# Hybrid decoder trunk, gated DeltaNet pairs: rows of the first pair fetched per head, pieces of the late gate product moved among the W and sample products

## The reference

```python
qkv = silu(causal_dwconv(h @ w_qkv, ...)); q, k = l2norm(q) * DK**-0.5, l2norm(k)
beta, g = sigmoid(ab[:8]), -exp(a_log) * softplus(ab[8:] + dt_bias)      # per head and token
# in chunks of 64 tokens (prompt) or 8 (sample), per head:
lmat = strict_lower(k_beta @ k.T * decay)
u, w = solve(lmat + I, [v*beta, k_beta*exp(gc)])                          # unit lower triangular
v_new = u - w @ S;  o = (q*exp(gc)) @ S + (q @ k.T * decay) @ v_new
S = S*exp(g_last) + (k*exp(g_last - gc)).T @ v_new
gate = silu(h @ w_g);  y = (rmsnorm(o) * gate) @ w_out
```

## Time and profile before

| | us |
|---|---|
| median of 3 runs | 1540.74 |
| lowest and highest run | 1536.88, 1546.56 |
| profiled execution, its own time | 1545.22 |
| its span, first to last instruction | 1543.5 |
| PE busy | 1513.7 (98%) |
| DVE, ACT, POOL busy | 796.0 (52%), 740.2 (48%), 1074.7 (70%) |
| mean granted TensorE clock | 0.986 |

### The profile page before, as it was taken

The page is one execution under the profiler, slowest core; times in us unless marked ns, Lnnn a source line. Parts: engine busy times, 40 slices in busy tenths (PEclk is TensorE's granted clock), DMA queues, the critical chain, the costliest instruction groups (busy, mean ns, idle before and its releaser), DMA issues.

```text
span 1543.5 us, 32205 instructions
## 1 busy us (share of the span) xinstructions
PE 1513.7 (98%) x10218; PEld 1475.3 (96%) x10218; DVE 796.0 (52%) x1788; ACT 740.2 (48%) x1412; POOL 1074.7 (70%) x1039
## 2 busy tenths in 40 slices
PE   9999999999999999999999999999899999999997
PEld 8999999998999999887999999999898899999997
DVE  4555554017555412996655531476767866555401
ACT  6654444445444434556644443457554535444332
POOL 5568887774776678984876767765656546777674
PEclk9999999999999999999999999999899989999999
DMA  6444444552544655221556545544422225444453
GB/s 241 123 135 146 157 153 145 149 159 83 163 140 159 160 149 172 83 83 60 166 157 163 146 128 150 177 149 123 138 89 88 81 82 180 150 149 149 119 153 109
DMA packets 88109, 212.47 MB, mean 138 GB/s; under 512 B 25600, under 2 KB 33312, under 8 KB 88032
## 3 DMA queue, kind: packets, MB, share of 16 engines
q1 hardware_dynamic: 88032, 211.49, 44.8%
HBM read 201.80 MB, written 9.66 MB: 137 GB/s over the span
## 4 chain that ended last, share of the span: by engine, by line
PE 88%; DVE 4%; issue 3%; POOL 2%; ACT 1%; DMA 1%; SPq 0%; DVEq 0%; POOLq 0%; ACTq 0%
PE bank L936 25%; PE bank L938 25%; PE bank L937 25%; PE bank L1339 2%; PE bank L1174 2%; PE bank L1350 1%; POOL wlo L639 1%; POOL wlo L641 1%; PE bank L1405 1%; PE bank L1290 1%; PE bank L1435 0%; DVE bank L2367 0%; DMA fst<-in_d_st 0%; PE bank L1199 0%; DMA tmp<-scr_g 0%
## 5 line engine op out<-in xcount | busy, mean ns | idle before, releaser
L639 POOL TENSOR_TENSOR wlo<-raw,whi 128x512 fp32r<-128x512 f32 (+3 forms) x394 | 452.4, 1148 | 376.6 <-ACT whi L1498 338.8
L936 PE MATMUL bank<-Gh,whi 128*128 128x320 f32 x1880 | 587.7, 313 | 3.1 <-DVE M L2349 2.0
L938 PE MATMUL bank<-Gh,wlo 128*128 128x320 f32 x1880 | 582.2, 310 | 0.0
L937 PE MATMUL bank<-Gl,whi 128*128 128x320 f32 x1880 | 582.0, 310 | 0.0
L641 POOL TENSOR_TENSOR wlo<-raw,whi 128x512 fp32r<-128x512 f32 (+3 forms) x394 | 473.2, 1201 | 0.0
L1498 ACT ACTIVATE whi<-raw 128x1024 fp32r<-128x1024 f32 (+3 forms) x396 | 370.6, 953 | 50.4 <-PE bank L938 37.4
L936 PEld LDWEIGHTS bank<-Gh,whi 128*128 128x128 f32 x1880 | 354.2, 188 | 5.4 <-DVE M L2349 2.2
L937 PEld LDWEIGHTS bank<-Gl,whi 128*128 128x128 f32 x1880 | 354.1, 188 | 1.1
L938 PEld LDWEIGHTS bank<-Gh,wlo 128*128 128x128 f32 x1880 | 353.9, 188 | 0.0
L936 PE MATMUL bank<-Hh,whi 128*128 128x320 f32 x912 | 283.7, 311 | 4.0 <-DVE Hl L2308 2.5
L938 PE MATMUL bank<-Hh,wlo 128*128 128x320 f32 x912 | 281.9, 309 | 0.0
(11 more groups left out here) (401 smaller groups left out, 1866.1 us busy)
## 6 DMA issues: line engine op xcount, KB each, us to landing
raw<-in_f_up SPq DMA_DIRECT2D x176, 512.0 KB, 3.4
raw<-in_f_down SPq DMA_DIRECT2D x64, 384.0 KB, 3.2
raw<-in_f_down SPq DMA_DIRECT2D x64, 320.0 KB, 3.2
raw<-in_c_pw SPq DMA_DIRECT2D x24, 512.0 KB, 3.6
raw<-in_a_in SPq DMA_DIRECT2D x16, 512.0 KB, 4.9
raw<-in_d_qk SPq DMA_DIRECT2D x16, 512.0 KB, 3.6
raw<-in_d_vg SPq DMA_DIRECT2D x16, 512.0 KB, 3.6
raw<-in_a_out SPq DMA_DIRECT2D x8, 512.0 KB, 3.5
```

The costliest lines, as they stand in the source:

```text
L639: pool.tensor_tensor(wlo[k][:, 0:half], raw[k][:, 0:half], whi[k][:, 0:half].bitcast(F32), ALU.subtract).then_inc(half_ready, 1)
L936: nc.tensor.matmul(dst, wh, h, start=start and n == 0, stop=False)
L937: nc.tensor.matmul(dst, wh, lo, start=False, stop=False)
L938: ins = nc.tensor.matmul(dst, wl, h, start=False, stop=stop and end and n == len(tiles) - 1)
```

## The change

Five things are moved.

1. **Rows.** For pair 0 the three row loads of head 0 wait for unit 10 of `d_vg`, those of head 1 for unit 11 (before: both for unit 11), and they stand ahead of the load of the first late gate's weights on SP. On ACT the high splits of units 10 to 12 stand at the end of the previous value instead of at the start of the next. The gate of head 6 is evicted and passed through silu after `differences` and `decays`.
2. **Gate pieces.** Of the 24 pieces per pair 16 instead of 24 are done by the end of the levels; four stand between the u products, two in each head's sample products.
3. **Banks.** Both heads' sample products and W of head 0 share bank 0; u of head 1 goes to bank 4, so that bank 5 belongs to the gate until its eviction.
4. **Eviction** of the gate (`late_evac`) moves from level 4 to the end of chunk step 2, and ACT's `gate_high`, `gated_late` move behind the next pair's `decays`.
5. **POOL.** `gate_low` moves from ahead of the state scaling to behind the sample spread (L753). In the last pair the split of the first `d_out` unit moves there too.

```diff
@@ SP
                         if x == 0:
                             sp.wait_ge(rows_stored, 48)
-                            sp.wait_ge(lo_ready, START["d_vg", 3] + 12)
+                        sp.wait_ge(half_ready, START["d_vg", 3] + 11 + x)
+                        sp.wait_ge(lo_ready, START["d_vg", 3] + 11 + x)
...
+                    gdn_row_loads(0)
                     load_gate(0)
-                    gdn_row_loads(0)
@@ POOL
-                if last:
-                    split_lo(START["d_out", 3] + 1, 1, UNIT)
-                else:
+                if not last:
                     scaled_keys(b + 1)
...
-                    gate_low(b + 1)
...
                                        ALU.mult).then_inc(vx_ready, 1)
+                if not last:
+                    gate_low(b + 1)
                 if not (isinstance(b, int) and b == 0):
                     head_lo(b * 2 - 2)
                 if last:
-                    for k in range(2, 4):
+                    for k in range(1, 4):
@@ PE
-                        gate(*((8, 9), (11, 12), (14, 15), (17, 18), (20, 24))[lev])
+                        gate(*((8, 9), (10, 11), (12, 13), (14, 15), (16, 16))[lev])
...
-                            gate(*((9, 11), (12, 14), (15, 17), (18, 20))[lev])
+                            gate(*((9, 10), (11, 12), (13, 14), (15, 16))[lev])
...
                         if x == 1:
-                            pe.wait_ge(late_evac, b + 1)
-                        nc.tensor.matmul(T(bb, 0), T(TT[x], 0), T(vp[x], 0), start=True, stop=True).then_inc(u_done, 1)
+                            gate(16, 20)
+                            pe.wait_ge(w_ready, b * 2 + 2)
+                        nc.tensor.matmul(T(bank[(1, 4)[x]], 0), T(TT[x], 0), T(vp[x], 0), start=True, stop=True).then_inc(u_done, 1)
...
+                            if s_ in (2, 5):
+                                at = 20 + 2 * x + s_ // 3
+                                gate(at, at + 1)
@@ ACT
-                    ring_hi(u0 + j + 3)
+                    if h < 5:
+                        ring_hi(u0 + j + 3)
...
+                    if 4 <= h < 7:
+                        ring_hi(u0 + j + 4)
...
                 values(0)
-                gate(6)
                 growth(0)
...
                 decays(0)
+                gate(6)
...
-                        gate_high(b + 1)
-                        gated_late()
                         values(b + 1)
                         decays(b + 1)
+                        gate_high(b + 1)
...
+                    gated_late()
@@ DVE
-                        if lev == 4:
-                            dve.wait_ge(late_done, b + 1)
-                            vec.tensor_tensor(tile_of(GT, b * 2 + 1), bank[5][:, 0:NT], R[:, :], ALU.mult).then_inc(late_evac, 1)
...
                             vec.tensor_copy(VNs[0][0:64, :], bank[0][0:64, P:2 * P]).then_inc(vns_ready, 1)
+                            dve.wait_ge(late_done, b + 1)
+                            vec.tensor_tensor(tile_of(GT, b * 2 + 1), bank[5][:, 0:NT], R[:, :], ALU.mult).then_inc(late_evac, 1)
```

More of the change, by code:

```diff
@@ L1377, in gdn_pair @@
                         if lev < 4:
-                            gate(*((9, 11), (12, 14), (15, 17), (18, 20))[lev])
+                            gate(*((9, 10), (11, 12), (13, 14), (15, 16))[lev])
                     for x in range(2):
-                        ba, bb, bc, bd = bank[4 * x:4 * x + 4]
+                        ba = bank[4 * x]
                         pe.wait_ge(inv_ready, b * 10 + (9 + x))
@@ L1386, in gdn_pair @@
                         ins.then_inc(w_done, 1)
+                    for x in range(2):
                         if x == 1:
-                            pe.wait_ge(late_evac, b + 1)
-                        nc.tensor.matmul(T(bb, 0), T(TT[x], 0), T(vp[x], 0), start=True, stop=True).then_inc(u_done, 1)
+                            gate(16, 20)
+                            pe.wait_ge(w_ready, b * 2 + 2)
+                        nc.tensor.matmul(T(bank[(1, 4)[x]], 0), T(TT[x], 0), T(vp[x], 0), start=True, stop=True).then_inc(u_done, 1)
                     for x in range(2):
@@ L1396, in samples_by_state @@
                     def samples_by_state(x):
-                        h, ba = b * 2 + x, bank[4 * x]
+                        h, ba = b * 2 + x, bank[0][:, 2 * P * x:2 * P * (x + 1)]
                         pe.wait_ge(w_ready, h + 1)
@@ L1409, in turn_samples @@
                     def turn_samples(x):
-                        nc.tensor.transpose(bank[4 * x][0:64, P:2 * P], vsT[x][:, 64:128], ident[:, :]).then_inc(vs_turned, 1)
+                        nc.tensor.transpose(bank[0][0:64, (2 * x + 1) * P:(2 * x + 2) * P], vsT[x][:, 64:128], ident[:, :]).then_inc(vs_turned, 1)
                     for c in range(1, CHUNKS):
@@ L1416, in gdn_pair @@
                             pe.wait_ge(vs_ready, b * 2 + 1)
+                        if c == 2:
+                            nc.tensor.matmul(T(bank[1], 2), T(TT[0], 1), T(vp[0], 1), start=True, stop=False)
+                            turn_samples(0)
                         if c < 3:
                             samples_by_state(c - 1)
-                        if c == 2:
-                            turn_samples(0)
                         for x in range(2):
-                            bb, bd = bank[4 * x + 1], bank[4 * x + 3]
-                            nc.tensor.matmul(T(bb, c), T(TT[x], t0), T(vp[x], t0), start=True, stop=False)
+                            bb, bd = bank[(1, 4)[x]], bank[4 * x + 3]
+                            if c != 2 or x == 1:
+                                nc.tensor.matmul(T(bb, c), T(TT[x], t0), T(vp[x], t0), start=True, stop=False)
                             pe.wait_ge(w_ready, b * 2 + (x + 1))
@@ L1434, in gdn_pair @@
                                 pe.wait_ge(vs_ready, b * 2 + 2)
+                                pe.wait_ge(vns_ready, b * 2 + 1)
                             nc.tensor.matmul(bc[:, 0:P], T(kdec[x], t0), T(VN[x], c), start=True, stop=True)\
@@ L1449, in gdn_pair @@
                         pe.wait_ge(vx_ready, h + 1)
+                        if x == 1:
+                            pe.wait_ge(late_evac, b + 1)
                         nc.tensor.matmul(bank[4 * x][:, :], T(kdec[x], 2)[0:32, :], VX[x][0:32, 0:512], start=True, stop=True)
@@ L2621, in gdn_pair @@
                             vec.tensor_copy(VN[x][r:r + CHUNK, c * P:(c + 1) * P],
-                                            bank[4 * x + 1][r:r + CHUNK, c * P:(c + 1) * P]).then_inc(vn_ready, 1)
+                                            bank[(1, 4)[x]][r:r + CHUNK, c * P:(c + 1) * P]).then_inc(vn_ready, 1)
                         if c == 0 and later:
@@ L2626, in gdn_pair @@
                             dve.wait_ge(vs_turned, b * 2 + 2)
-                            vec.tensor_copy(VNs[1][0:64, :], bank[4][0:64, P:2 * P]).then_inc(vns_ready, 1)
+                            vec.tensor_copy(VNs[1][0:64, :], bank[0][0:64, 3 * P:4 * P]).then_inc(vns_ready, 1)
                         for x in range(2):
@@ L2645, in gdn_pair @@
                             dve.wait_ge(sv_done, b * 2 + (x + 1))
-                            vec.tensor_copy(vsT[x], bank[4 * x][:, 0:P]).then_inc(vs_ready, 1)
+                            vec.tensor_copy(vsT[x], bank[0][:, 2 * P * x:2 * P * x + P]).then_inc(vs_ready, 1)
                         if c == 2:
```

1 line of the change is left out of this document (removed).

## The result

| | before | changed |
|---|---|---|
| median of 20 runs, us | 1541.41 | 1546.80 |
| lowest and highest, us | 1536.88, 1547.21 | 1543.51, 1549.51 |
| profiled execution: own time, span, us | 1545.22, 1543.5 | 1548.02, 1546.5 |
| mean granted clock in it | 0.986 | 0.990 |

The ratio is 1.003, with a 95% interval of 1.0019 to 1.0040. The forecast of no change within 1% held, and so did its range (1531 to 1549). But the interval excludes equality: the change costs about 5 us (2.9 to 6.2), where the sum said 0.1, and the median lies 6 us above the 1540.8 that was named. So the working has to be gone through step by step.

A forecast was written before the change was run, and what follows sets the result against it. TensorE, busy 98% of the span, was taken to bound the kernel. The terms -8.1 + 3.7 + 1.0 + 5.3 - 1.8 = +0.1 us gave 1545.3 profiled, 1540.8 on the median, range 1531 to 1549.

The forecast's parts named there:

- two of the rivals, at 1545.6 and 1549: Gate load landing late at pair 0's start (1545.6, chance 0.15); clock falls staying or moving (1549, chance 0.15).
- Step 1: TensorE's clock in pairs 1 to 3: wide pieces among the sample products remove the falls to 1.2 GHz, -8.1 us.
- Step 2: Gate pieces moved from the levels to the u and sample products: net cost over four pairs, +3.7 us.
- the stretch from head 1's samples to step 3: Sign of being right: sample products to chunk step 3 take near 4.3 + 0.5 us in all pairs.
- Step 3: VectorE's gate eviction ahead of the v_new copies of chunk step 3: 0.25 us per pair, +1.0 us.
- Step 4: Pair ends: POOL's `gate_low` beside VectorE's queries makes the second query wait, +5.3 us.
- the queries escape: Pair ends: VectorE's queued second query gets in before `gate_low`, total -3.4 us, 1537; chance 0.25.
- The row that carried the step, 0.34 us: Ahead of pair 0, a VectorE key product ended 0.34 us after `gate_low`, read as waiting for POOL's instruction end.
- Step 5: Start of pair 0: rows issued earlier per head, gate load behind them landing at about 1098, -1.8 us.
- the gate's load lands late: Start of pair 0: load lands 7.1 us or more after issue, +3 instead of -1.8, 1545.6; chance 0.15.
- Priced at nothing: ACT's extra table load, pair 3's extra POOL split and later SP gate loads were counted as costing no time.
- it pays where it was aimed: Whole kernel: falls gone, start at -5, moved pieces at 0, giving 1533; chance 0.1.

The follow-up runs named there:

- g4: Kernel before, unchanged, profiled a second time; it and h3 took 1541.77 and 1542.14 us.
- h3: Kernel before, unchanged, profiled a third time; g4 and it took 1541.77 and 1542.14 us.
- g2: Kernel before with only the change's new start of pair 0, gate load still ahead of the rows; 1540.07 us, ratio 0.9993 to the kernel before.
- h4: Changed kernel, unchanged, profiled once more; 1544.83 us.
- f1: Changed kernel with the first gate load issued ahead of pair 0's row loads on SP; 1544.22 us, ratio 1.0005 to the kernel before.
- f4: Changed kernel with the gate pieces among the sample products put back between the u products; 1558.26 us, ratio 1.0103 to the kernel before.
- f3: Changed kernel with POOL's `head_lo` first, then `gate_low` behind a wait for DVE's queries; 1541.55 us, ratio 0.9992 to the kernel before.
- f2: Changed kernel with POOL's low part of the gate's weights cut into four instructions of 256 columns; 1545.44 us, ratio 1.0018 to the kernel before.
- g1: Changed kernel with both f1's earlier gate load and f3's POOL order; 1539.82 us, ratio 0.9986 to the kernel before.
- h1: Changed kernel with all four gate pieces of the sample stretch among head 1's sample products; 1548.08 us, ratio 1.0048 to the kernel before.
- g3: Changed kernel with each head's two gate pieces right ahead of its sample products instead of among them; 1546.21 us, ratio 1.0035 to the kernel before.
- h2: Changed kernel with all four gate pieces of the sample stretch among head 0's sample products; 1545.46 us, ratio 1.0026 to the kernel before.

## Why the prediction was right, and where its working was not

"No change within 1%" held because 5 us are 0.35% of this kernel, and the range because it was 18 us wide. The number named was 6 us off; two of the rivals, at 1545.6 and 1549, stood closer.

**Step 1 failed, in its size.** The falls went, as forecast: -8.1 us between the profiled executions. (Which of the moves took them away isn't isolated; see below.) But the sum was made against one execution and carried to the median by a constant ("the median of the runs is 1540.7, which is 4.5 lower"). Those 4.5 us were no constant: that execution was slower than most for a reason inside the term itself, the 4.9 us of pair 3's long fall, which g4, h3 and g2 don't have. By these executions a typical run of the kernel before loses 3.2 us to the falls in its pairs, and that is all that their removal gives back. With -3.2 in place of -8.1, and the other four steps as measured, the sum is -3.2 + 2.9 + 1.0 + 4.8 + 0.2 = +5.7 us, and +5.4 was measured, with 2.9 to 6.2 as its interval: the agreement is closer than either number is known. Most directly, the stretch from the mask transposes to the next layer is 173.95 us in h4 and 168.6 in g4 and h3, 5.35 more. The mean clock of whole executions can't decide between 3.2 and 8.1: it is 0.9878 before (29 runs beside f1 to f4) and 0.9914 changed (20 runs), the 29 go by 1.3 us for each 0.001 (an estimate from a line through them), which makes 4.7 us, but the two profiled executions, 0.986 and 0.990, differ by as much with 8.1 us in the pairs, because falls elsewhere count in it too.

**Step 2 held** (+2.9 for 3.7). Pair 0 cost 0.7, pairs 1 and 2 0.6 to 0.7 each, pair 3 0.9. The levels gave back 0.30 us in pairs 1 to 3, as counted, and 0.5 instead of 1.0 in pair 0. What was too dear is the pieces: 1.2 us for the eight, 0.15 each wherever they stand, and not 1.6. Head 1's sample products show it; to the product behind them they took 1180.94 - 1178.94 = 2.00 us, and before, to this row of TensorE's timeline, 1175.20 - 1173.45 = 1.75:

```profile
1175.20 0.45 PE L1406 MATMUL bank<-Hl_spare,M 128*128 128x64 f32 x2
```

The working also missed the sixth move. By it the stretch from head 1's samples to step 3, for which the prediction gave 4.3 + 0.5 us as a sign, took 1183.20 - 1178.94 = 4.26 in pair 1.

**Step 3 held**: 0.26 us per pair, +1.0.

**Step 4 held**, and was the cost that mattered: +4.8 for 5.3. The query pair took 3.37 us, and f3 gave back 3.7 us of pair ends by order alone, the other 1.1 going into the smaller collision. The rival "the queries escape" fell in all pair ends of the changed kernel. The row that carried the step, 0.34 us, was enough. As the Trainium skill has it (SBUF — State Buffer, Who interferes with whom), the port that VectorE's second input shares with POOL is locked for an instruction, not shared by the cycle; f2 agrees, since quarters of the same work cut the queries from 3.37 to 1.74 us.

**Step 5 failed**: +0.2 for -1.8. (Over all executions: 15.4 us on average in three of the kernel before, 14.9 in seven that have the changed kernel's start, 13.8 to 16.0. That is a gain of 0.5 us, well inside the spread; with it the sum above is +5.0.) Less the 1.8 us by which the whole place lies later, the gate's load was issued at 1092.9 and in ACT's hands at 1098.7, where I had 1092.8 and 1098. From there to TensorE's first key product I had summed 4.9 us of lengths, and it took 1106.30 - 1100.51 = 5.8, above all because POOL's first key row took 1.44 us beside DVE's differences, for the 0.9 counted. So TensorE started at 1104.5 for 1103, and reached the product that had stood at 1106.57 at 1107.1 for 1105.7; the clock then gave back 0.4 us for 0.9. This is the rival "the gate's load lands late" in a mild form. f1, g1 and g2 show what the rows per head are worth when the load goes first: 3.1 to 3.8 us against the starts of the kernel before.

**"Priced at nothing"** stands: nothing of it appeared in a stage.

So the range held, with two misses of +4.9 and +2.0 us that its width covered, and two terms 0.8 and 0.5 too dear. (A slip in the sums: the rival "it pays where it was aimed" comes to 1533.9, not 1533.) The expected gain of the clock was not given back anywhere: as far as four executions tell, three fifths of it did not exist in a typical run.

What stays open is the condition for a fall. Counted over the profiles, with pieces in the sample stretch 2 of 36 passes of a pair fell (f1 in pair 3, f2 in pair 0; nine executions); without them pairs 1 and 2 fell in 10 of 10 passes, which all hold a wait of 0.39 us or more at the chunk step, and pairs 0 and 3, which hold none, in 2 of 10. So a fall came each time that the wait and the bare stretch stood together, in 2 of 10 passes with the bare stretch alone, and in neither of h1's two with the wait alone. That is a count and not a mechanism. With the pieces the sixth move, the u products and the eviction changed place too; f4 shows that these alone aren't enough, and no run shows whether they are needed. The Trainium skill (TensorE: Matmul & The Clock Gate, Part 1) ties the low state to how busy the engine was; here the engine was held up for 0.39 us in pairs 1 and 2, and four passes of a pair fell with no wait on record at all, so gaps alone don't explain it.

## What to carry to other kernels

Before a gain is counted that lies in a granted clock, profile two or three executions: a fall that is in every one is worth its time, one that is in a single profile may be absent from the median already. Put a long instruction of POOL where VectorE's two-input operations are not, and order it by a wait rather than by cutting it, unless POOL's own queue has slack. When loads are split to come sooner, ask what stands behind them in the same queue; here the order of two lines decided whether the split gave 3 us at this place or next to nothing.

## What the runs showed that was not expected

- Runs of one kernel differ mostly by their clock: 29 runs of the kernel before cover 1537.59 us at a mean of 0.991 to 1548.29 us at 0.984, and the line through them takes up four fifths of the variance. One run beside h1 doesn't fit at all, 1539.4 us at 0.941.
- Cutting one POOL instruction of 1024 columns (2.60 us) into four costs POOL 0.7 us and gives DVE 1.6.
- The start of pair 0 takes 13.8 to 16.0 us in seven executions of kernels that are the same up to there (changed, h4, g3, h1, h2, f3, f4: 15.87, 14.98, 15.23, 15.98, 14.56, 14.03, 13.83); stretches at 1.2 GHz of 7 to 10 us lie in it in all, and no run here separates them from the landing of the loads.
